# One gathered tile's sums moved from the dense v phase to a longer gate phase, and the v phase reordered around deeper buffers

## What is computed

```python
q = (xf @ w_pq).reshape(t, PEER_HEADS, 2, PEER_HALF)
s = jnp.einsum('thpd,hpkd->thpk', q, sub_keys)
sv, si = lax.top_k(s, PEER_TOPK)            # then the best 16 of the 256 pairs: gv, idx
g = jax.nn.softmax(gv, axis=-1)
u = expert_u[idx_blk]
a = g_blk * jax.nn.gelu(jnp.einsum('tkd,td->tk', u, x_blk), approximate=False)
ff = jnp.einsum('tk,tkd->td', a, expert_v[idx_blk])
h = layer_norm(DN_ALPHA * h + ff, ln3_g, ln3_b)
```

## Time and profile before

| | us |
|---|---|
| median of three runs (3690.63 to 3697.85) | 3696.43 |
| the profiled execution, its own time | 3706.79 |
| its span, first to last instruction | 3705.0 |
| phase A, about 1270 to 2285 | 1015 |
| gate phase, 2285 to 2645 | 360 |
| dense v phase with the end, 2645 to 3705 | 1060 |

### The profile page before, as it was taken

One profiled execution on the slowest core, in us unless ns is written; L12 is line 12 of the kernel. 1 busy time (PEld: TensorE's weight loads), 2 busy tenths in 40 slices (PEclk: granted clock), 3 DMA queues, 4 the chain that ended last, 5 costly groups with the idle time before them and its releaser, 6 DMA issues. The chain is left out here.

```text
span 3705.0 us, 42794 instructions
## 1 busy us (share of the span) xinstructions
PE 3103.8 (84%) x16184; PEld 2401.6 (65%) x16184; DVE 2125.5 (57%) x4487; ACT 1195.2 (32%) x1931; POOL 1444.6 (39%) x1116
## 2 busy tenths in 40 slices
PE   4995989688979899999999997666478778899994
PEld 3874777677768778887777765444256556566663
DVE  4134774215422358988777876666366566555555
ACT  3112551304121134343333334887221121222221
POOL 2101002500210025656767766776444444322222
PEclk9996799798989899999999998888699889999997
DMA  4333012422222368998999998999999999988883
GB/s 153 104 104 119 1 55 88 136 76 87 88 86 80 103 217 335 365 347 333 410 410 410 406 412 323 366 388 384 357 339 327 332 331 338 329 309 307 312 309 142
DMA packets 368045, 937.45 MB, mean 253 GB/s; under 512 B 31440, under 2 KB 130264, under 8 KB 366816
## 3 DMA queue, kind: packets, MB, share of 16 engines
q0 software_dynamic: 147456, 536.94, 38.2%
q1 hardware_dynamic: 220384, 397.77, 30.5%
HBM read 827.60 MB, written 106.98 MB: 252 GB/s over the span
## 5 line engine op out<-in xcount | busy, mean ns | idle before, releaser
L1406 POOL DMA_INDIRECT ex_ring<-in_expert_v,ex_idxT_sb x406 | 448.1, 1104 | 485.3 <-PE ex_ps_v L1431 363.5
L1406 POOL DMA_INDIRECT ex_ring<-in_expert_u,ex_idx_sb x322 | 410.8, 1276 | 427.3 <-DVE ex_hg L1415 239.5
L1415 DVE CUSTOM_DVE_ANT_0 ex_ring<-ex_ring,ex_xg 128x1024 f32<-128x1024 f32 x322 | 384.9, 1220 | 111.7 <-DMA ex_ring<-in_expert_u,ex_idx_sb 83.3
L106 PE MATMUL eo_ps<-eo_v_hi_sb,aT_late_hi 128*128 128x512 f32 x1024 | 409.6, 400 | 46.5 <-DVE aT_late_lo L1979 46.5
L1431 PE MATMUL ex_ps_v<-ex_ring,ex_w_sb 128*32 128x512 f32 x1624 | 267.2, 703 | 191.3 <-DMA ex_ring<-in_expert_v,ex_idxT_sb 147.6
L106 PE MATMUL ex_ps_h<-aT_late_hi,ex_uT_hi_sb 128*128 128x512 f32 x1024 | 414.4, 405 | 12.9 <-ACT ex_act L1559 8.0
L108 PE MATMUL ex_ps_h<-aT_late_hi,ex_uT_lo_sb 128*128 128x512 f32 x1024 | 403.1, 394 | 0.0
L107 PE MATMUL ex_ps_h<-aT_late_lo,ex_uT_hi_sb 128*128 128x512 f32 x1024 | 401.8, 392 | 0.0
L107 PE MATMUL eo_ps<-eo_v_lo_sb,aT_late_hi 128*128 128x512 f32 x1024 | 401.6, 392 | 0.0
L108 PE MATMUL eo_ps<-eo_v_hi_sb,aT_late_lo 128*128 128x512 f32 x1024 | 400.0, 391 | 0.0
L1986 DVE TENSOR_TENSOR eo_acc<-eo_acc,eo_ps 128x1024 f32<-128x1024 f32 x124 | 151.4, 1221 | 419.4 <-PE eo_ps L108 266.1
(11 more groups left out here) (328 smaller groups left out, 6613.6 us busy)
## 6 DMA issues: line engine op xcount, KB each, us to landing
ex_u_raw<-in_expert_u SPq DMA_DIRECT2D x128, 512.0 KB
eo_v_raw<-in_expert_v SPq DMA_DIRECT2D x128, 512.0 KB
act_d<-ex_act SPq DMA_DIRECT2D x128, 256.0 KB
gate_d<-ex_gate SPq DMA_DIRECT2D x8, 4096.0 KB
eo_g_raw<-gate_d SPq DMA_DIRECT2D x64, 512.0 KB
eo_a_raw<-act_d SPq DMA_DIRECT2D x128, 256.0 KB
h_d<-n_row SPq DMA_DIRECT2D x24, 512.0 KB, 2.6
pin_raw<-in_w_in SPq DMA_DIRECT2D x20, 512.0 KB
```

What stands on the lines that cost most here:

```text
L106: pe.matmul(ps, l_hi, r_hi, start=first, stop=False)
L1406: pool.indirect_dma_start(rows(n), None, table, bass.IndirectOffsetOnAxis(at, 0)).then_inc(ring_in[slot[n]], 16)
L1415: dve.tensor_tensor_reduce(out=u, in0=u, in1=xg[:, j, :], scale=1.0, scalar=0.0, op0=ALU.mult, op1=ALU.add, accum_out=hg[:, j, k:k + 1]).t ...
```

## The change

1. **The sums of tile 2 move.** The gate phase goes from 72 to 96 steps and takes the v gathers of tiles 1 and 2 (256 in place of 128). Its 64 dots now all stand in the first 40 steps. Tile 1's sums end by step 46; at step 48 (TURN_G) DVE adds tile 1's residual and spreads tile 2's weights; tile 2's sums fill steps 50 to 95. The dense phase keeps 128 v gathers (tile 3), in steps e 68 to 111.
2. **Dots of the dense phase** stand in steps 0 to 59 in place of 0 to 63.
3. **Parked tiles.** The finished tiles 0 and 1 are stored to DRAM at the start of the dense phase (the buffer `h0_d`, free by then), and their SBUF rows serve as two more activation buffers and one more v buffer: four and three deep. The first four steps load into buffers of their own. The two tiles come back near the end, into ring slots that are free.
4. **Order on DVE**: `multiply` one step ahead, then `low_parts` before `add`. Each dense tile's residual row is loaded into `eo_acc` first, and the first `add` folds it in (one instruction in place of a copy, and none at the end).
5. **Norms inside.** Tiles 2, 3, 0, 1 are normalised within groups 30 and 31; tiles 4 to 7 each behind their last sum.
6. **Phase A**: tile 0's keys are picked one step sooner, and every gathered tile's indices are ready before the softmax of its gates is waited for; dots begin at e = 9 in place of 12 (352 as before).

```diff
-            STEPS_G = HOT_GROUPS + 8
+            STEPS_G, TURN_G = HOT_GROUPS + 32, 48
-            FIRST_DOT = 12
+            FIRST_DOT = 9
-            VALS_A, VALS_G, VALS_B = P, P, 2 * P
+            VALS_A, VALS_G, VALS_B = P, 2 * P, P
+            LAST_VALS, LN_TILES = 112, GROUPS - 2
+            A_SLOTS, V_SLOTS = 4, 3
+            def dots_g(n):
+                first = 2 * (DOTS_G // 2)
+                return share(first, TURN_G - 8, n) if n < TURN_G - 8 else 0
+            def vals_g(n):
+                if n < TURN_G - 2:
+                    return share(P // 4, TURN_G - 2, n)
+                if n >= TURN_G + 2:
+                    return share(P // 4, STEPS_G - TURN_G - 2, n - TURN_G - 2)
+                return 0
+            def dots_b(e):
+                return share(DOTS_B, ETILES // 2 - 4, e) if e < ETILES // 2 - 4 else 0
+            def vals_b(e):
+                half = ETILES // 2
+                if half + GE <= e < LAST_VALS:
+                    return share(P // 4, LAST_VALS - half - GE, e - half - GE)
+                return 0
...
+                            for j in range(2):
+                                sp.wait_ge(sum_g, j + 1)
+                                sp.dma_start(kept[j * P:(j + 1) * P, :], xg[:, j, :]).then_inc(kept_out[j], 16)
+                            for e in range(GE, ETILES):
+                                if e >= GE + A_SLOTS:
+                                    sp.wait_ge(a_lo_done, e - A_SLOTS + 1)
...
+                                if e >= GE + V_SLOTS:
+                                    sp.wait_ge(v_lo_done, e - V_SLOTS + 1)
...
                                 if q == 0:
-                                    dve.tensor_copy(acc[:, t, :], ps[t % 2][:]).then_inc(added[t % 2], 1)
+                                    dve.wait_ge(row_in[t], 16)
+                                    dve.scalar_tensor_tensor(acc[:, t, :], acc[:, t, :], ALPHA, ps[t % 2][:], ALU.mult, ALU.add).then_inc(added[t % 2], 1)
...
-                            for q in range(GROUPS + 1):
+                            for q in range(GROUPS):
                                 for x in range(GE):
-                                    if q < GROUPS:
-                                        multiply(q * GE + x)
+                                    if q * GE + x + 1 < ETILES:
+                                        multiply(q * GE + x + 1)
+                                    low_parts(q * GE + x)
                                     if q >= 1:
                                         add(q - 1, x)
-                                    if q < GROUPS:
-                                        low_parts(q * GE + x)
...
+                                    if LN_TILES <= q < LN_TILES + GT // 2:
+                                        j = 2 * (q - LN_TILES) + x // 2
+                                        if x % 2 == 0:
...
+                                            ln.statistics(dve, j, whole_row(j))
+                                        else:
+                                            ln.scale(dve, j)
+                                        if x % 2 == 0 and j >= 1:
+                                            ln.times_gain(dve, j - 1, whole_row(j - 1))
```

More of the change, by code:

```diff
@@ L1311, in expert_stages @@
             for n in range(STEPS_G):
-                for _ in range(share(DOTS_G, STEPS_G, n)):
+                for _ in range(dots_g(n)):
                     gathers.append(("u", nu))
                     nu += 1
-                for _ in range(4 * share(VALS_G // 4, STEPS_G, n)):
+                for _ in range(4 * vals_g(n)):
                     gathers.append(("v", nv))
@@ L1318, in expert_stages @@
             END_G = len(gathers)
-            for n in range(GE * (GROUPS + 1)):
-                for _ in range(share(DOTS_B, ETILES // 2, n) if n < ETILES // 2 else 0):
+            for e in range(ETILES + GE):
+                for _ in range(dots_b(e)):
                     gathers.append(("u", nu))
                     nu += 1
-                for _ in range(4 * share(VALS_B // 4, ETILES, n - GE) if n >= GE else 0):
+                for _ in range(4 * vals_b(e - GE)):
                     gathers.append(("v", nv))
@@ L1368, in expert_stages @@
             row_in = [sem(f"eo_row_in{i}") for i in range(DT)]
-            sum_done, stored = sem("eo_sum"), sem("eo_stored")
+            first_in = [sem(f"eo_first_in{i}") for i in range(GE)]
+            kept_out, kept_in = [[sem(f"eo_kept_{w}{i}") for i in range(2)] for w in ("out", "in")]
+            stored = sem("eo_stored")
             with ExitStack() as whole:
@@ L1666, in route @@
                                                                ginv[:].unsqueeze(2).broadcast_to([P, PH, TOPK]), ALU.mult))
[L1667 to L1673, removed]
+                                    dve.wait_ge(chain, m)
                                     dve.sem_inc(route_done, 1)
@@ L1855, in _ @@
                                         one_hot(n + 2)
-                                    for _ in range(share(DOTS_G, STEPS_G, n)):
+                                    for _ in range(dots_g(n)):
                                         dot(dve, done)
                                         done += 1
-                                weigh(dve, 2)
+                                    if n == TURN_G - 3:
+                                        weigh(dve, 2)
+                                    if n == TURN_G:
+                                        add_residual(dve, 1)
+                                        spread_weights(dve, 2)
                             @block.tensor
@@ L1878, in _ @@
                                         gates(n)
-                                    for _ in range(share(VALS_G // 4, STEPS_G, n)):
+                                    if n == TURN_G:
+                                        weight_transpose(pe, 2)
+                                    for _ in range(vals_g(n)):
                                         values(pe, done)
@@ L1884, in expert_stages @@
                     sb, pb = local(stage)
-                    ln = RowNorm("eo_ln", sb, gain, bias, rows=(spreads[:, 0, :], spreads[:, 1, :]))
+                    ln = RowNorm("eo_ln", sb, gain, bias, rows=(ring[:, 2, :], ring[:, 3, :]))
                     acc = sb("eo_acc", [P, DT, D])
@@ L1929, in _ @@
                                     sp.wait_ge(val_done, GT * P // 4)
                                     ln.load(sp)
-                            for j in range(TT):
-                                sp.wait_ge(ln.ln_done, j + 1)
-                                sp.dma_start(dest[j * P:(j + 1) * P, :], whole_row(j)).then_inc(stored, 16)
+                                    for j in range(2):
+                                        sp.dma_start(ring[:, j, :], kept[j * P:(j + 1) * P, :]).then_inc(kept_in[j], 16)
@@ L1934, in _ @@
+                            for n in range(TT):
+                                j = NORM_ORDER[n]
+                                sp.wait_ge(ln.ln_done, n + 1)
+                                sp.dma_start(dest[j * P:(j + 1) * P, :], whole_row(n)).then_inc(stored, 16)
                             sp.wait_ge(stored, 16 * TT)
@@ L2022, in _ @@
+                            for t in range(DT):
+                                add(GROUPS - 1, t)
+                                dve.wait_ge(added[t % 2], 2 * (GROUPS - 1) + t // 2 + 1)
+                                ln.statistics(dve, GT + t, whole_row(GT + t))
+                                ln.times_gain(dve, GT + t - 1, whole_row(GT + t - 1))
+                                ln.scale(dve, GT + t)
                             ln.times_gain(dve, TT - 1, whole_row(TT - 1))
@@ L2044, in _ @@
                                     last.then_inc(out_mm[t % 2], 1)
-                                    for _ in range(share(VALS_B // 4, ETILES, q * GE + t)):
+                                    for _ in range(vals_b(q * GE + t)):
                                         values(pe, done)
```

142 lines of the change are left out of this document (87 added, 55 removed).

## The result

| | us |
|---|---|
| changed kernel, median of four (3625.37 to 3632.35) | 3631.88 |
| kernel before, median of four in the same timing | 3694.58 |
| ratio | 0.983, 95% interval 0.981 to 0.984 |
| span of the profiled execution | 3630.0 (3705.0 before) |

The medians are 63 us apart, the two profiled spans 75, since the profiled execution of before lay some 12 us over its median. On another chip the same changed kernel was at 0.987 of the kernel before (50 us). The forecast of 3667 was too high, by 35 us, and it had the gain at less than half of what came: 29 us for 63.

What follows compares the result with a forecast made beforehand. Transfers were taken to bound most of the last 2300 us. Terms -6 + 183 - 5 - 164 - 37 = -29 us took the span from 3705 to 3676, adjusted to a 3667 us median; range 3612 to 3712, forecast's own 3640 to 3685.

Steps and rivals of the forecast that it cites:

- The prediction's own sign of being wrong: Signs listed beforehand: a gate step over 8.4 us, a first-part dense group over 25, or a middle group near 28.
- What bounds the kernel now: Last 2300 us: mostly transfers; dense second half at PE's own pace, 27.25 us a group; 155 us to be won.
- Price of a transfer: Gate phase: 1.39 us a gather; dense phase: 1.45 us a gather and 12.3 us of loads a group.
- The step that failed: Dense groups 17 to 27: transfers of 29.2 us over a share of 0.96 give 30.4 a group, 334 us.
- the dense term: All 32 dense groups: 815 us where PE needed 979 before, so -164 us.
- Phase A: Phase A: ten dots go ahead of step 12, saving six gathers at 1.28 us, -6 us.
- Gate phase: Gate phase with 96 steps: 543 us, so +183 us; steps 0 to 39 at 7.7 us each, 308 us.
- GpSimd as the bound: Gate steps 0 to 39: gathers that meet DVE make GpSimd the limit, 9.5 us a step, 3739 us; chance 0.14.
- Start: Barrier to PE's dense start: buffers for all four first steps cut 29 us to 24, -5 us.
- End: Behind the last PE matmul: one add and the last norm's remainder, 13.4 us in place of 50.7, -37 us.
- The first rival: Dense phase: deeper buffers let transfers run at share 1.03 and groups reach PE's pace, 3613 us; chance 0.2.
- The second rival: From the gate phase on: DMA share stays at 0.89, each phase trading waits, 3693 us, no change; chance 0.14.

Runs made afterwards that it cites:

- e13: The changed kernel with 40 more stores to unused DRAM rows, four in each of dense groups 18 to 27; 0.993, 3682 us.
- e14: e12 with six of the eight gather ring slots used in the dense phase; 1.015, 3772 us.
- e4: The changed kernel with DVE's old order in the dense phase, deeper buffers kept; 1.017, 3773 us.
- e6: The kernel before with only the moved sums (change 1), two-deep buffers and old order kept; 1.025, 3801 us.
- e10: The changed kernel with 20 more stores to unused DRAM rows, two in each of dense groups 18 to 27; 0.985, 3639 us.
- e8: The changed kernel with its four inner norms spread over 12 steps in place of 8, each engine's part a step behind the part it waits for; 0.982, 3640 us.
- e1: The kernel before with only the phase A edit (change 6); 0.999, 3699 us.
- e2: e1 with dots beginning at step 12, as in the kernel before; 1.001, 3709 us.
- e7: The changed kernel, nothing edited, timed again on the same chip as e1, e2 and e8; 0.987, 3657 us.
- e9: e8 with no dots in the first dense group and step 3's low parts ahead of step 4's multiply; 0.977, 3613 us.
- e12: The changed kernel with spread norms as in e8 and tile 2's sums back in the dense phase, gate phase of 72 steps; 0.979, 3616 us.

## Why the prediction was off, step by step

In the profiled pair the span is 46 us under the forecast's 3676. The dense groups make up 24 of them, phase A 14, the gate phase 12 and what runs ahead of phase A 3, while the start of the dense phase came 8 longer than forecast. The prediction's own sign of being wrong came: a middle group near 28.

**What bounds the kernel now.** "The last 2300 us are mostly a question of transfers" was wrong for the dense phase. There a DMA share of 0.94 went with 333 GB/s, and the same queues moved 405 GB/s in e13, though with stores among them; what holds the mixed first half at 345 is in part the ring (e14). The second half's 27.25 us were called PE's own pace, split as 21.9 + 4.1 + 1.2. The 21.9 holds (groups 16 and 28 of the changed kernel), but the old order's turn costs some 4.8 us where no `values` call fills it (e4, e6). The sum came out right since the change removes the whole turn, whatever its size.

**Price of a transfer.** A busy share over a count gave 1.45 us a gather and 12.3 us a group, and these were added up and divided by 0.96. Busy share isn't additive: with 5.5 MB more in 240 us it rose by 0.03, not by the 0.06 those bytes take at 410 GB/s. The Trainium skill ("DMA: Bandwidth & Descriptors", Specifications) puts the fabric's ceiling at 435 GB/s; no 40 us window of these traces is over 419, so no run here reaches it.

**The step that failed.** "Transfers: 12.3 + 11.6 x 1.45 = 29.2, over 0.96 = 30.4" for groups 17 to 27. They take 307 us for 334 (28.1 in ten of them, against PE's 27.9): -27, where the dense term as a whole was off by -24. The step took the transfers for the limit and 0.96 for the most that their share can reach. The share reached 1.01, at which the 29.2 would be 28.9 us and not 30.4, and even there it wasn't the limit: a tenth more bytes cost 3% more time (e10). By bytes the group needs an estimated 10.3 MB / 410 = 25.1 us. What sets its length is PE, which is busy for all but 0.13 of the 308 us. The rest of that term: groups 0 to 15 -8 (22.5 for 23.0, the same error), groups 28 to 31 +12. There the prediction gave "1 us for the norms between", and ACT's and DVE's waits for each other cost 13 (e8).

**Phase A.** -6 was forecast; e1 measured -8.5 by its medians, with an interval wide enough for 0 and for -12, and its trace -12. The mechanism fits too, dots ahead of step 12 and not the early gathers (e2). Whether the further 8 to 12 us of the profiled pair are the change's stays open; the spread of the other traces is larger than that.

**Gate phase.** +183 forecast, +170 in the first pair; by the gates' matmuls steps 0 to 39 took 284 us for 308, steps 40 to 63 114 for 111, and steps 64 to the end 127 for 116. In the first 40 steps GpSimd issued 164 gathers where these steps use up 172: at least eight had been issued before, which the sum didn't take off, by its own prices 12 of the 24 us (an estimate; no run tried it). With the start of the dense phase it is +173 and, by e7, +184 us, for a forecast of +178: no error beyond what chips differ by.

**GpSimd as the bound** (third rival) didn't come: a gate step took 7.1 us, a gather 1.29 us of GpSimd on average in those steps, as forecast. DVE and GpSimd do hold each other up: the low part of 3.42 us above began 0.44 us behind a GpSimd add of 2.77 and ended 1.1 behind that add's end, as if it ran only then. That is the rule of the Trainium skill ("SBUF — State Buffer", SBUF: two separate sides) that one of the two gets the port pair for the whole instruction; the trace agrees, and e8 shows that it decided nothing here.

**Start.** -5 was forecast, +2.7 came. Most loads were in place, but five dots and a multiply that waits 2.3 us for a gate load stood ahead of the low parts of step 3 (e9 gives 6 us of it back).

**End.** -37 forecast, -37.5 measured.

**The first rival** (dense phase at PE's pace, 3613), given 0.2, was nearer in each phase: 22 and 28.5 us a group for 22.5 and 28.1 measured, and a gate phase of 525 for 531. Its reason was half right: the share did rise, to 1.01 for its 1.03, but it was not what held the groups back, and depth alone gives nothing (e4). Against its 3613 the norms took some 12 us more and the start 8, and phase A 14 less. That 3632 lies in the wider range, 3612 to 3712, is owed to this rival, which set the lower end; the forecast's own range, 3640 to 3685, missed it.

**The second rival** (the share stays at 0.89, no change) didn't come: from the gate phase on it is 0.92, 336 GB/s in place of 322.

## What to carry to other kernels

Price transfers in bytes over the best rate seen, not in busy share: here a share of 1.01 still hid a tenth more. That gives a least time only; the mixed half never came near it. A loop through two engines has a length of its own; find it by listing what stands between the end of one group and the start of the next, and look for a turn that other work doesn't fill, since such work hides its true size. Depth and order belong together: an order that makes loads urgent needs the buffers that make them early, and before work is moved to another phase, compare what it costs there with what it frees here: beside the other edits the moved sums came out even.

## What was unexpected

- The new order with two-deep buffers is slower than the old order with them: 28.1 against 26.3 us a group.
- Where the DMA share already read 1.01, 10.5 MB more of stores cost 8 us, and 21 MB cost 23.
- The same instructions in phase A took from 998 to 1034 us in fourteen traces, while two traces of the same dense phase were 3 us apart (791 and 794).
- All edits but the moved sums, with the spread norms, give 0.979 (e12); with the moved sums they give 0.982 (e8, another chip).
